# First projection: x read in a transposed layout, the norm's factors multiplied in place

## The reference

```python
xn = rms_norm(h, ln_g)            # xf * rsqrt(mean(xf*xf) + EPS) * g, over 1024 values
proj = xn @ w_in
qkv_a, a_raw, b_raw, z_a, q_b, k_b, v_b, z_b = jnp.split(proj, split_at, axis=-1)
# qkv_a: causal convolution of width 4 over frames, silu, then the gated delta rule (group A)
# q_b, k_b, v_b: chunk-band attention (group B); then an output projection and a gated embedding
```

## Time and profile before

| | us |
|---|---|
| median of 3 runs | 3682.59 |
| lowest and highest run | 3674.52, 3691.48 |
| profiled execution, first to last instruction | 3678.1 |
| TensorE busy in it | 3394.7 (92%) |
| VectorE busy | 2181.8 (59%) |
| ScalarE busy | 1388.4 (38%) |
| GpSimd busy | 979.1 (27%) |

### The profile page before, as it was taken

One profiled execution on the slowest core, in us unless ns is written; L12 is line 12 of the kernel. 1 busy time (PEld: TensorE's weight loads), 2 busy tenths in 40 slices (PEclk: granted clock), 3 DMA queues, 4 the chain that ended last, 5 costly groups with the idle time before them and its releaser, 6 DMA issues. The chain is left out here.

```text
span 3678.1 us, 69025 instructions
## 1 busy us (share of the span) xinstructions
PE 3394.7 (92%) x26606; PEld 2899.7 (79%) x26606; DVE 2181.8 (59%) x4410; ACT 1388.4 (38%) x2650; POOL 979.1 (27%) x1281
## 2 busy tenths in 40 slices
PE   7999999969998999998787567999997999999998
PEld 6999899957877888886777455888885888888887
DVE  7777687747987968761556455666664322323332
ACT  5555455533223323211555324666663111111111
POOL 3222122228996644400666400000000000000000
PEclk9999999979999999998999788999998999999999
DMA  5433333345337453434765543222225121212121
GB/s 157 116 105 105 107 108 112 89 149 152 127 103 227 133 158 103 123 105 142 250 209 191 135 139 124 73 76 85 73 70 175 56 74 56 69 60 68 61 69 36
DMA packets 320478, 420.06 MB, mean 114 GB/s; under 512 B 189923, under 2 KB 212739, under 8 KB 315574
## 3 DMA queue, kind: packets, MB, share of 16 engines
q1 hardware_dynamic: 320190, 416.17, 36.7%
HBM read 259.25 MB, written 159.46 MB: 114 GB/s over the span
## 5 line engine op out<-in xcount | busy, mean ns | idle before, releaser
L88 PE MATMUL b_psP<-b_w_hi,b_xT_hi 128*128 128x512 f32 x1320 | 518.9, 393 | 38.5 <-DVE b_xT_lo L1319 21.8
L89 PE MATMUL b_psP<-b_w_lo,b_xT_hi 128*128 128x512 f32 x1320 | 516.8, 391 | 0.0
L90 PE MATMUL b_psP<-b_w_hi,b_xT_lo 128*128 128x512 f32 x1320 | 516.5, 391 | 0.0
L88 PE MATMUL a_psG<-a_xT_hi,a_w_hi 128*128 128x256 f32 (+1 forms) x1536 | 453.6, 295 | 21.0 <-DVE a_xT_lo L668 19.5
L89 PE MATMUL a_psG<-a_xT_lo,a_w_hi 128*128 128x256 f32 (+1 forms) x1536 | 441.3, 287 | 0.0
L90 PE MATMUL a_psG<-a_xT_hi,a_w_lo 128*128 128x256 f32 (+1 forms) x1536 | 440.6, 287 | 0.0
L88 PEld LDWEIGHTS a_psG<-a_xT_hi,a_w_hi 128*128 128x128 f32 x1536 | 294.9, 192 | 42.6 <-DVE a_xT_lo L668 23.5
L88 PEld LDWEIGHTS b_psP<-b_w_hi,b_xT_hi 128*128 128x128 f32 x1320 | 249.8, 189 | 97.7 <-DVE b_xT_lo L1319 45.6
L685 DVE SCALAR_TENSOR_TENSOR a_act<-a_raw,a_taps,a_act 128x256 f32<-128x256 f32 x576 | 289.1, 502 | 20.6
L89 PEld LDWEIGHTS a_psG<-a_xT_lo,a_w_hi 128*128 128x128 f32 x1536 | 295.3, 192 | 0.0
L90 PEld LDWEIGHTS a_psG<-a_xT_hi,a_w_lo 128*128 128x128 f32 x1536 | 295.3, 192 | 0.0
(11 more groups left out here) (368 smaller groups left out, 7493.7 us busy)
## 6 DMA issues: line engine op xcount, KB each, us to landing
rows_b<-b_rows SPq DMA_DIRECT2D x165, 256.0 KB, 2.1
b_x_full<-xT SPq DMA_DIRECT2D x78, 512.0 KB, 4.3
qkvB<-a_act SPq DMA_DIRECT2D x16, 1536.0 KB, 5.4
d_conv_T<-qkvB SPq DMA_DIRECT2D x16, 1536.0 KB, 10.7
xT<-a_x_full SPq DMA_DIRECT2D x33, 512.0 KB, 3.6
h_mixed<-mixed SPq DMA_DIRECT2D x33, 512.0 KB, 4.0
out<-h_y SPq DMA_DIRECT2D x33, 512.0 KB, 2.9
a_x<-in_x_prompt SPq DMA_DIRECT2D x32, 512.0 KB, 4.4
```

Of the source, the lines that this page charges most:

```text
L88: nc.tensor.matmul(out, x_hi, w_hi, start=first, stop=False)
L89: nc.tensor.matmul(out, x_hi, w_lo, start=False, stop=False)
L90: return nc.tensor.matmul(out, x_lo, w_hi, start=False, stop=last)
```

## The change

The host lays out x a second time: for each tile of 128 rows, the 128x128 squares are transposed, so that a plain load gives x with its columns on the partitions. `load_xT` loads it straight into `x_full`, which has three buffers now (`XBUFS`). The rows of x are still loaded, for the sum of squares only, and have one buffer; `load_x` waits for the `square` of the tile before it. ScalarE's `scale` is gone. GpSimd multiplies x_full by the channel gain in place (`channel_gain`). TensorE's eight transposes of a tile become one (`spread`): the column of 128 row factors, broadcast to 128x128, is transposed into one bank of PSUM, `psB`, so that every partition holds all the row factors. VectorE's `full` multiplies x_full by them in place. At the start `channel_gain(1)` and `norm(1)` follow GpSimd's third weight split, and `square(1)` follows ScalarE's sixth.

```diff
-    RING, SLOTS = 6, 7
+    RING, SLOTS, XBUFS = 6, 7, 3
...
-        x_raw = [ph.sb(f"a_x{i}", [P, D]) for i in range(2)]
+        x_raw = ph.sb("a_x", [P, D])
         squares = ph.sb("a_squares", [P, D], mybir.dt.bfloat16)
-        x_full = [ph.sb(f"a_x_full{i}", [P, KT, P]) for i in range(2)]
+        x_full = [ph.sb(f"a_x_full{i}", [P, KT, P]) for i in range(XBUFS)]
...
-        psT = ph.ps("a_psT", [P, KT * P])
+        psB = ph.ps("a_psB", [P, 512])
...
             def load_x(t):
-                if t >= 2:
-                    sp.wait_ge(xT_ps, t - 1)
+                if t:
+                    sp.wait_ge(ssq_ok, t)
                 src = d.x_p[order[t] * P:(order[t] + 1) * P, :] if t != SAMPLE else d.x_s
-                sp.dma_start(x_raw[t % 2][:, :], src).then_inc(x_in[t % 2], 16)
+                sp.dma_start(x_raw[:, :], src).then_inc(x_in, 16)
+
+            def load_xT(t):
+                if t >= XBUFS:
+                    sp.wait_ge(spilled[t % XBUFS], 16 * (t // XBUFS))
+                    sp.wait_ge(lo_ok, t - XBUFS + 1)
+                    sp.wait_ge(ab_ok, t - XBUFS + 1)
+                src = d.xT_p[order[t] * P:(order[t] + 1) * P, :] if t != SAMPLE else d.xT_s
+                sp.dma_start(x_full[t % XBUFS][:, :, :], src.rearrange("p (k n) -> p k n", k=KT)).then_inc(xT_in[t % XBUFS], 16)
 
             def spill(t):
                 sp.wait_ge(full_ok, t + 1)
-                sp.dma_start(d.xT[order[t]], x_full[t % 2][:, :, :]).then_inc(spilled[t % 2], 16)
+                sp.dma_start(d.xT[order[t]], x_full[t % XBUFS][:, :, :]).then_inc(spilled[t % XBUFS], 16)
...
             load_x(0)
+            load_xT(0)
             with nc.allow_non_contiguous_dma(reason="small per-channel constants, once"):
                 sp.dma_start(lnT[:, :], d.ln_g.rearrange("(k p) -> p k", p=P)).then_inc(ln_in, 16)
-            load_x(1)
+            load_xT(1)
...
+                if m == 4:
+                    load_x(1)
                 if m == 16:
                     load_x(2)
+                    load_xT(2)
                     spill(0)
                 if m == 20:
-                    load_x(3)
                     spill(1)
             for b in range(BLOCKS):
...
-                    if t + 2 < TILES:
-                        load_x(t + 2)
+                    if t + 1 < TILES:
+                        load_x(t + 1)
+                        load_xT(t + 1)
                     spill(t)
...
+            def channel_gain(t):
+                x = x_full[t % XBUFS]
+                pool.wait_ge(xT_in[t % XBUFS], 16 * (t // XBUFS + 1))
+                pool.tensor_tensor(x[:, :, :], x[:, :, :], lnT[:, :].unsqueeze(2).to_broadcast([P, KT, P]), ALU.mult)\
+                    .then_inc(gained, 1)
...
+            pool.wait_ge(ln_in, 16)
+            channel_gain(0)
             norm(0)
-            norm(1)
             for i in range(HALVES // 2):
                 lo_part(pool, 2 * i + 1, w_lo_g)
+                if i == 2:
+                    channel_gain(1)
+                    norm(1)
...
                         norm(ahead[0])
+                        channel_gain(ahead[0])
                     if g == 5 and len(ahead) > 1:
                         norm(ahead[1])
...
-            def scale(t):
-                e.wait_ge(rstd_ok, t + 1)
-                e.activation(x_raw[t % 2][:, :], x_raw[t % 2][:, :], ACT.Copy, scale=rstd[:, t % 2:t % 2 + 1]).then_inc(scaled, 1)
...
             square(0)
-            square(1)
-            scale(0)
             hi_part(0)
             hi_part(1)
-            scale(1)
             for m in range(2, HALVES):
                 hi_part(m)
                 if m == 4:
                     split_hi(0)
-                if m == 8:
+                if m == 5:
+                    square(1)
+                if m == 9:
                     split_hi(1)
...
-            def transposes(t):
-                pe.wait_ge(scaled, t + 1)
+            def spread(t):
+
+                a = t % 2
+                pe.wait_ge(rstd_ok, t + 1)
                 if t:
                     pe.wait_ge(full_ok, t)
-                for k in range(KT):
-                    last = nc.tensor.transpose(psT[:, k * P:(k + 1) * P], x_raw[t % 2][:, k * P:(k + 1) * P], ident[:, :])
-                last.then_inc(xT_ps, 1)
+                nc.tensor.transpose(psB[:, 0:P], rstd[:, a:a + 1].to_broadcast([P, P]), ident[:, :]).then_inc(rstd_ps, 1)
...
             def full(t):
-                v.wait_ge(xT_ps, t + 1)
-                if t >= 2:
-                    v.wait_ge(spilled[t % 2], 16 * (t // 2))
-                    v.wait_ge(lo_ok, t - 1)
-                    v.wait_ge(ab_ok, t - 1)
-                v.tensor_tensor(x_full[t % 2][:, :, :], psT[:, :].rearrange("p (k n) -> p k n", k=KT),
-                                lnT[:, :].unsqueeze(2).to_broadcast([P, KT, P]), ALU.mult).then_inc(full_ok, 1)
+                x = x_full[t % XBUFS]
+                v.wait_ge(gained, t + 1)
+                v.wait_ge(rstd_ps, t + 1)
+                v.tensor_tensor(x[:, :, :], x[:, :, :], psB[:, 0:P].unsqueeze(1).to_broadcast([P, KT, P]), ALU.mult)\
+                    .then_inc(full_ok, 1)
```

More of the change, by code:

```diff
@@ L187, in project_a @@
         w_lo_g = ph.sem("a_w_lo_g")
-        x_in = [ph.sem(f"a_x_in{i}") for i in range(2)]
+        x_in = ph.sem("a_x_in")
         ssq_ok = ph.sem("a_ssq_ok")
@@ L191, in project_a @@
         rstd_ok = ph.sem("a_rstd_ok")
-        scaled = ph.sem("a_scaled")
-        xT_ps = ph.sem("a_xT_ps")
+        xT_in = [ph.sem(f"a_xT_in{i}") for i in range(XBUFS)]
+        gained = ph.sem("a_gained")
+        rstd_ps = ph.sem("a_rstd_ps")
         full_ok = ph.sem("a_full_ok")
@@ L212, in project_a @@
         ab_s = ph.sem("a_ab_s")
-        spilled = [ph.sem(f"a_spilled{i}") for i in range(2)]
+        spilled = [ph.sem(f"a_spilled{i}") for i in range(XBUFS)]
         stored = [ph.sem(f"a_stored{i}") for i in range(2)]
@@ L428, in _ @@
                         norm(ahead[0])
+                        channel_gain(ahead[0])
                     if g == 5 and len(ahead) > 1:
                         norm(ahead[1])
+                        channel_gain(ahead[1])
                     if g == 8 and len(ahead) > 2:
                         norm(ahead[2])
+                        channel_gain(ahead[2])
                     if g == 8:
@@ L525, in _ @@
                             square(ahead[0])
-                        if g == 1:
-                            scale(ahead[0])
                         if g == 4:
@@ L584, in gate_product @@
                     for x in range(PARTS):
-                        last = nc.tensor.matmul(psAB[PCOLS * x:PCOLS * (x + 1), at], w_ab[:, k0 + x, :], x_full[t % 2][:, k0 + x, :],
+                        last = nc.tensor.matmul(psAB[PCOLS * x:PCOLS * (x + 1), at], w_ab[:, k0 + x, :], x_full[t % XBUFS][:, k0 + x, :],
                                                 start=k0 == 0, stop=k0 + PARTS == KT)
@@ L610, in query_sums @@
                 last.then_inc(rows_ps, 1)
-            transposes(0)
-            transposes(1)
+            spread(0)
+            spread(1)
             for b in range(BLOCKS):
@@ L631, in _ @@
                     if g == 3 and ahead:
-                        transposes(ahead[0])
+                        spread(ahead[0])
                     if g == 8 and len(ahead) > 1:
-                        transposes(ahead[1])
+                        spread(ahead[1])
                     if g == 10 and len(ahead) > 2:
-                        transposes(ahead[2])
+                        spread(ahead[2])
                     for t in product_at.get((b, g), ()):
@@ L667, in split_lo @@
                 v.wait_ge(hi_ok, t + 1)
-                v.tensor_tensor(xT_lo[b % 2][:, :, a * P:(a + 1) * P], x_full[t % 2][:, :, :],
+                v.tensor_tensor(xT_lo[b % 2][:, :, a * P:(a + 1) * P], x_full[t % XBUFS][:, :, :],
                                 xT_hi[b % 2][:, :, a * P:(a + 1) * P].bitcast(F32), ALU.subtract).then_inc(lo_ok, 1)
@@ L3362, in build, with columns_first, laid_out @@
     combine(nc, d, s)
+def columns_first(rows):
+    T, N = rows.shape
+    tiles = np.reshape(rows, (T // P, P, N // P, P))
+    return np.ascontiguousarray(np.transpose(tiles, (0, 3, 2, 1)).reshape(T, N))
+def laid_out(inputs, s):
+    out = {}
+    out["xT_p"] = columns_first(inputs["x_prompt"][0])
+    out["xT_s"] = columns_first(np.reshape(inputs["x_sample"], (s.DECB * s.DECT, s.D)))
+    return out
 def sizes(inputs):
@@ L3396 @@
     outs = [nc.dram_tensor(f"out_{i}", shape, F32, kind="ExternalOutput").ap() for i, shape in enumerate(outputs)]
-    build(nc, args[:-1], outs, s, args[-1])
+    laid = laid_out(inputs, s)
+    columns = {name: nc.dram_tensor(f"in_{name}", a.shape, F32, kind="ExternalInput").ap() for name, a in laid.items()}
+    arrays.update({f"in_{name}": a for name, a in laid.items()})
+    build(nc, args[:len(INPUTS)], outs, s, args[-1], columns)
```

17 lines of the change are left out of this document (7 added, 10 removed).

## The result

| | us |
|---|---|
| after, median of 16 runs | 3698.01 (3689.14 to 3705.08) |
| before, median of 16 runs beside it | 3683.22 (3674.52 to 3693.56) |
| ratio | 1.0038, 95% interval 1.0029 to 1.0047 |
| profiled execution after, first to last instruction | 3690.1 (before 3678.1) |

No change in the sense of the prediction (within 0.5%, 18 us), but the median is 14.8 us up where 2 were forecast. Each run's time is 1.8 us above its own span, so the profiled executions were quick ones on both sides.

A forecast was written before the change was run, and what follows sets the result against it. A chain through VectorE, 13.2 us from group 7's rows to `split_lo`, was taken to bound the steady block, nearly tied with TensorE. Terms 1 + 3 + 1 - 3.0 = +2 on 3682.59 gave 3685 us, range 3667 to 3704.

The forecast's parts named there:

- the likeliest case: Whole kernel: no change, 3685 us with a spread of 3674 to 3696; chance 0.59.
- First transposes: Steady block, after group 3: seven of eight transposes go, group 4's rows come 0.75 us earlier on the chain.
- Second transposes: Steady block, after group 8: 0.75 us saved on TensorE only, off the chain, lengthening its wait.
- Second gain: Steady block, beside group 5's convolution: a 1.9 us GpSimd product blocks its last tap, ending it 1.8 us late.
- Behind it silu, and group 7's rows: Steady block, after group 5's late tap: 234.41 - 1.89 + 1.9 = 234.4, so the boundary stays, 0.0 a block.
- rival 4: Block boundaries: TensorE's clock falls after longer waits, +30 us over 11 blocks, 3715; chance 0.04.
- The wait grows to 2.0, below both: Steady boundaries: TensorE's wait of 2.0 us stays below the 2.59 (rate held) and 4.47 (clock 0.50) seen before.
- Block 0: First block: both gains block VectorE nearly in full, 1.9 us for the second and about 1.3 for the first: +3.
- I cost it at nothing: SP and DMA: second tile's later loads, x without slack and transposed x with 2 us, were priced at zero.
- rival 3: Second tile of a block: with one x buffer the load comes too late, +20 us, 3705; chance 0.14.
- but the next block's wait for the stores absorbs it: Block 0 to 1: TensorE's clock falls in block 0 after a wait of about 5 us, at no net cost.
- Blocks 8 and 9: These blocks are TensorE's: four groups of transposes saved, 4 x 0.75 = -3.0 us.

The follow-up runs named there:

- experiment 7: Changed kernel with every row factor's transpose made eight times, at both places of a block; 3691.47 us, ratio to before 1.0022.
- 3: Changed kernel with only the second tile's row-factor transpose of each block made eight times; 3685.89 us, ratio to before 1.0010.
- 8: Changed kernel with the first tile's gain cut to 128x8 in blocks 1 to 15; 3695.13 us, ratio to before 1.0036.
- 4: Changed kernel with the second tile's gain at group 2, its load issued earlier (blocks 1 to 14 without 9); 3672.42 us, ratio to before 0.9976.
- 2: Changed kernel with no channel gain at all, outputs lacking it; 3666.62 us, ratio to before 0.9956.
- 5: Changed kernel with the second gain at group 2 (blocks 2 to 7, 10 to 14) and tile 3 loaded early; 3669.74 us, ratio to before 0.9962.
- 6: Changed kernel with twelve useless identity transposes in TensorE's wait at the end of blocks 1 to 14; 3688.27 us, ratio to before 1.0011.
- 9: Changed kernel with tile 3 loaded early and block 0's two gains cut to 128x8; one run, 3689.67 us.
- 1: Changed kernel with both loads of tile 3 issued during block 0's weights, at piece 26; 3694.26 us, ratio to before 1.0033.

## Why the forecast was right in kind and short in size

The median, 3698.0, lies in the stated range (3667 to 3704) but above what the likeliest case alone was to give (3674 to 3696), and "no change" held with 3.6 us to spare. The steady blocks came out by the mechanism forecast. The rest of the 14.8 us did not, and that it stayed within 18 is in part luck.

- **The steady blocks: right, step by step.** First transposes 0.76 on the chain (experiment 7 against 3; 0.75 forecast). Second transposes off it (3). First gain nothing (8). Second gain 1.9 us long and serial with the taps (profile after). With both sets of transposes back a block is 44.43; before it was 43.90 with `scale`'s 1.14 in the chain; so the gain costs 0.53 more than `scale` did. Timelines of these two kernels (7 and before) show each size. Silu of group 5 comes 1.51 later in the block (28.67 against 27.16 us from its start): that is the gain beside the taps, 3.04 - 1.53. From there to group 7's rows it is 2.05 instead of 3.09: `scale` was worth 1.04, not 1.14. Behind the rows 0.06 are lost, so the gain costs 1.57, where 1.9 stood in the sum. 0.76 + 1.04 - 1.57 = 0.23 is what the blocks came out shorter than the forecast's 0.0.
- **"Behind it silu, and group 7's rows"** is confirmed by taking it away: with the gain at group 2 the block is 42.1 (4), with none too (2). 25.6 us of the 31.4 between the changed kernel and the one without gains lie in where one GpSimd instruction a block stands, the clock that held at the boundaries included.
- **TensorE's clock, rival 4: a term left out.** The step that failed is "The wait grows to 2.0, below both". The rows showed a wait of 2.59 after which the rate held, and I took waits below it as safe, and gave the fall 0.04 as all or nothing. It fell at 11 of 29 boundaries with waits of 1.81 to 1.93 us, and at none with 1.2 or less (3, 7) or 0.2 to 0.5 (2, 4, 5, 6). The price was off as well: 2.9 us each was taken, 1.5 is measured. Freeing TensorE lengthened its wait and cost 5 us at the steady boundaries by the traces. The medians of 3 and 6 say 10 to 12, with uncertainties of some 5; what they have beyond the 5 isn't assigned.
- **Block 0: +3 forecast, +7 measured.** The gains are 3.3 of it, as priced (9). Two terms were missing. One is the load: "I cost it at nothing" was argued from the steady block, where the transfer does land in time, but in block 0 the issue stood behind the weights and the second tile was late. This is rival 3's mechanism in a single place, 1 to 2 us (1). The other is the clock. The forecast had it fall here and went on "but the next block's wait for the stores absorbs it". It cost 1.9 us behind the last wait of the block, and of the whole 6.9 us by which block 1 began late its wait for `a_kq` took up 0.7 (1.88 instead of 2.59). 0.7 us stay unassigned.
- **Block 1: 0.0 forecast, +0.55 measured** (47.09 against 46.54). The clock fell behind that wait of 1.88. In the three traces in which it held there (3, 6, 7) the block took 44.8 to 45.1 us, with its wait at 1.23 or less.
- **Rival 3 elsewhere**: no wait above 0.8 us, but for one landing in twelve traces of one-buffer kernels, 3.3 us (6). It is a tail, not the case.
- **Blocks 8 and 9: -3.0 forecast, -1.0 measured** to block 11. "Four groups of transposes" were saved, but TensorE then met the next engine: its waits for ScalarE's row sums grew from 0.43 to 1.20, a wait of 1.45 for `a_kq` is new, and at block 11's start it stands 1.81 instead of 0.51. A block in which TensorE never waits has other chains just behind.
- **Start (+1) and block 7 (+1)**: measured -0.1 and +0.1.
- **The base of the sum**: 4.5 us between span and median were carried over. 1.8 of it belongs to every run; the rest was that execution's luck.
- **Open**: the 3.6 us of the profiled span behind the first load of `project_b`. Three executions of the changed kernel have 3.6, 14.2 and 1.0 us there against the one of before, and the experiments 1.3 to 11, in no order that follows the edits. The profiles can't assign it; the medians contain it.

## What to carry to other kernels

Price a GpSimd pass at the place where it falls: the same 1.9 us cost some 1.6 a block beside the taps that a tight chain runs through, and nothing three groups earlier, beside taps with idle time behind them. Moving one call (and its load) was worth 26 us here, some 5 of them because the clock no longer fell at the boundaries. When an engine is freed that isn't the bound, look at what its longer idle time does: TensorE lost to its clock about as much as it gained, if not more. With all its old work given back (7) the median is 6.5 us lower, with intervals that overlap a little, and useless transposes alone brought back 9.7 (6). A cost argued to be nothing from the steady state has to be argued again for the first round, where the queues are still full of weights.

## What the hardware showed that was not expected

- TensorE's clock fell behind 11 of 29 boundary waits of 1.81 to 1.93 us, for about 1.5 us of loss each, and behind none of 1.2 us or less, although in the kernel before it had held through a wait of 2.59 us. The same place keeps the rate in one execution and loses it in the next. Behind `a_kq` it fell once after 1.45 us only (8, block 10, at 508.0), and in block 1 it fell in all nine traces after the change with waits of 1.68 to 3.74 us there, in none of the three with 1.23 or less. So the length of the wait alone doesn't decide between 1.45 and 2.59.
- A 1.90 us GpSimd product added 1.5 us to three VectorE taps (3.04 against 1.53), and delayed a 16x256 operation of 0.41 us to 2.14 when `a_qsq` ran at the same time.
- GpSimd's 128x1024 product in place took 1893 to 1898 ns in all 33 cases. By the Trainium skill (GPSIMD Engine Reference, "Elementwise — side-by-side cycle accounting") half of its 4497 ns for 2048 would be an estimated 2.25 us; the measurement is 16% below it and decides.
